# Streaming encoder step: weight products by pairs of column groups, and a dense weight matrix laid out for direct use as stationary operand

## The reference, cut to what matters

```
z = rmsnorm(x) @ w_in; h = x + mixers(z) @ w_out        # retention and mLSTM heads
q = rmsnorm(h) @ w_q;  s1, s2 = q against keys1, keys2   # 8 heads, 128 keys each
pick 16 best (i1, i2) pairs per head -> expert e = i1 * 128 + i2, with a gate
h += sum over picked e of gate * gelu(u[e] . x) * v[e]   # 128 experts per token, of 16384
h += sigmoid(rmsnorm(h) @ w_ple_gate) * (p @ w_ple_proj); y = rmsnorm(h)
```

## Time and profile before

| | |
|---|---|
| time, three runs | 3791.88, 3810.11, 3811.25 us; median 3810.11 |
| the profiled execution: its time, its span | 3817.56 us, 3815.7 us |
| mean granted TensorE clock | 0.899 |
| PE busy | 3148.9 us (83%) |
| DVE busy | 2762.2 us (72%) |
| ACT, POOL busy | 679.6 us (18%), 1329.1 us (35%) |
| moved | 1470.90 MB, mean 385 GB/s |

### The profile page before, as it was taken

How to read it: one execution, slowest core, us unless ns; L and a number is a source line. 1 busy time by engine, 2 the same in 40 slices (tenths; PEclk the granted TensorE clock), 3 DMA queues, 4 the chain that set the end, 5 groups by cost and what they waited for, 6 DMA issues and landing times.

```text
span 3815.7 us, 27395 instructions
## 1 busy us (share of the span) xinstructions
PE 3148.9 (83%) x9486; PEld 1696.0 (44%) x9486; DVE 2762.2 (72%) x3853; ACT 679.6 (18%) x1648; POOL 1329.1 (35%) x905
## 2 busy tenths in 40 slices
PE   8998697998885559999888645699999999888927
PEld 4447343544464234454437635344444444343403
DVE  1005987677677778878757788878788999787772
ACT  2212110222020221123202457000000000011003
POOL 0001533224235444423333522433333333246460
PEclk9999798999997769999998756899999999998968
DMA  7889999999999999999899999999999999999995
GB/s 268 283 274 342 418 417 418 417 418 419 416 398 414 390 362 417 417 417 397 328 402 408 377 365 337 357 420 420 420 420 420 420 419 412 411 417 397 413 370 185
DMA packets 333059, 1470.90 MB, mean 385 GB/s; under 512 B 28152, under 2 KB 66488, under 8 KB 198712
## 3 DMA queue, kind: packets, MB, share of 16 engines
q0 software_dynamic: 129744, 944.82, 60.6%
q1 hardware_dynamic: 192528, 512.40, 35.3%
q10 hardware_dynamic: 10648, 11.92, 1.0%
HBM read 1443.36 MB, written 25.69 MB: 385 GB/s over the span
## 4 chain that ended last, share of the span: by engine, by line
DMA 41%; PE 24%; DVE 9%; issue 5%; POOL 5%; ACT 3%; SPq 0%; DVEq 0%; ACTq 0%; POOLq 0%
DMA ring<-in_peer_v,eidx 21%; PE psum L830 13%; DMA ring<-in_peer_u,eidx 9%; POOL ring L766 5%; DMA W<-in_w_peer_q 5%; PE psum L808 4%; DVE ring L2135 3%; DVE arena L2147 3%; PE psum L1076 2%; PE psum L1139 2%; DMA a_scratch<-arena 1%; DMA W<-in_w_out 1%; DMA W<-in_w_ple_gate 1%; PE psum L1109 1%; PE psum L1194 1%
## 5 line engine op out<-in xcount | busy, mean ns | idle before, releaser
L766 POOL DMA_INDIRECT ring<-in_peer_u,eidx x576 | 879.6, 1527 | 1739.4 <-DVE dots L2135 1310.1
L2135 DVE CUSTOM_DVE_ANT_0 ring<-ring,cx 128x2048 f32<-128x2048 f32 x576 | 1312.1, 2285 | 207.5 <-DMA ring<-in_peer_u,eidx 205.5
L2147 DVE SCALAR_TENSOR_TENSOR arena<-ring,wts,arena 128x2048 f32<-128x2048 f32 x320 | 751.8, 2349 | 210.7 <-DMA ring<-in_peer_v,eidx 194.4
L830 PE MATMUL psum<-W,actT 128*128 128x512 f32 x1792 | 785.9, 597 | 14.0 <-DVE arena L1891 10.6
L766 POOL DMA_INDIRECT ring<-in_peer_v,eidx x320 | 446.3, 1395 | 632.6 <-DVE arena L2147 595.1
L830 PEld LDWEIGHTS psum<-W,actT 128*128 128x128 f32 x1792 | 339.7, 192 | 428.2 <-issue 417.2
L1139 PE MATMUL psum<-arena 128*128 128x512 f32 x1024 | 455.2, 605 | 22.1 <-DVE arena L2058 22.1
L808 PE MATMUL psum<-W,actT 128*128 128x512 f32 x960 | 432.3, 607 | 40.1 <-issue 28.0
L1139 PE MATMUL psum<-W,arena 128*128 128x512 f32 x1024 | 447.2, 596 | 8.7 <-DVE arena L2058 8.7
L1076 PE MATMUL psum<-actT,W 128*128 128x128 f32 (+2 forms) x1536 | 289.9, 354 | 82.8 <-DMA W<-in_w_peer_q 71.4
L1139 PEld LDWEIGHTS psum<-arena 128*128 128x128 f32 x1024 | 197.6, 195 | 269.6 <-issue 239.4
(11 more groups left out here) (283 smaller groups left out, 2149.1 us busy)
## 6 DMA issues: line engine op xcount, KB each, us to landing
W<-in_w_in SPq DMA_DIRECT2D x168, 1024.0 KB, 12.8
W<-in_peer_v SPq DMA_DIRECT2D x64, 1024.0 KB, 14.9
arena<-in_peer_v SPq DMA_DIRECT2D x64, 1024.0 KB, 17.6
W<-in_w_out SPq DMA_DIRECT2D x48, 1024.0 KB, 13.0
W<-in_w_peer_q SPq DMA_DIRECT2D x48, 1024.0 KB, 23.0
W<-in_w_ple_gate SPq DMA_DIRECT2D x48, 1024.0 KB, 16.3
actT<-a_scratch SPq DMA_DIRECT2D x64, 256.0 KB, 26.7
ring<-in_peer_u,eidx POOLq DMA_INDIRECT x576, 16.3
```

What stands on the lines that cost most here:

```text
L766: pool.indirect_dma_start(ring[:, slot, :], None, a["peer_u" if what == "u" else "peer_v"][0], off(ix, 0)).then_inc(ring_in[slot], 16)
L830: ins = pe.matmul(bank(4 * s + j), lhs(at_k, j), w_pair(q)[:, k, s * CG:(s + 1) * CG], start=(at_k == 0), stop=(at_k == KT - 1))
L2135: dve.tensor_tensor_reduce(row, row, cx[:, :], 1.0, 0.0, ALU.mult, ALU.add, dots[:, n % DEEP, c:c + 1]).then_inc(u_used, 1)
L2147: dve.scalar_tensor_tensor(out=hslot(t), in0=ring[:, slot, :], scalar=wts[:, n % DEEP, c:c + 1], in1=hslot(t), op0=ALU.mult, op1=ALU.add). ...
```

## The change

Five edits. `q` of g = 1, 2 and `ple` of e = 0, 1 are done by pairs too, with their places on ACT and DVE moved to where both groups of a pair are done (`done_at`, `group_at`, and the first pick from 1.5 to 2.6 units behind the start of `q`). The turned last quarter of `h` goes to other banks (`h_bank`). The operands of the build product change sides, so that A has the second index on partitions. A is written by transfers of 1 MB (16 tokens, two stages), in a scratch layout of 16 chunks, each with 8 KB in a piece for every second index; a chunk of 8 first indices is read back by one transfer of 1 MB. The dense product takes its stationary operand straight from the chunk, with a step of 8 elements (32 bytes) between tokens; transposes and their copies are gone.

```diff
-CHUNK = 4
+CHUNK = 8
+NCHUNK = NKEY // CHUNK
+WRITE = 4
...
 def paired(what, g):
-    return g > 0 and what in ("in", "out")
+    return g < 2 if what == "ple" else g > 0
...
     if i == j == 0:
-        return q_at(g, 1.5) + FIRST_PICK[g] * x
+        return q_at(g, 2.6) + FIRST_PICK[g] * x
...
 def group_at(e, i, x):
-    return embed_at(e, 4 + 2.2 * len(EMBEDS[e]) * (i + 1)) + x
+    n = len(EMBEDS[e])
+    if paired("ple", e):
+        return embed_at(e, 4 + 2.2 * n * (2 * (i // 2) + 2)) + n * (i % 2) + x
+    return embed_at(e, 4 + 2.2 * n * (i + 1)) + x
...
-        a_keep = nc.dram_tensor("a_scratch", (TOKENS, NKEY * NKEY), F32, kind="Internal").ap()
+        a_keep = nc.dram_tensor("a_scratch", (NCHUNK, NKEY, TOKENS, CHUNK), F32, kind="Internal").ap()
...
-                sp.wait_ge(a_c, b + 1)
-                sp.dma_start(a_keep[b * BATCH:(b + 1) * BATCH, :].rearrange("t (i k) -> i t k", i=NKEY),
-                             a_stage(b).rearrange("p (t k) -> p t k", t=BATCH)).then_inc(a_out[b % 4], 16)
+                sp.wait_ge(a_c, WRITE * (w + 1))
+                t0 = w * WRITE * BATCH
+                sp.dma_start(a_keep[:, :, t0:t0 + WRITE * BATCH, :].rearrange("c i t k -> i c (t k)"),
+                             a_stage(w).rearrange("p c t k -> p c (t k)")).then_inc(a_out[w % 2], 16)
...
                     if c >= 2:
-                        sp.wait_ge(at_tr, (c - 1) * CHUNK // VT)
-                    for b in range(len(DENSE)):
-                        sp.dma_start(a_chunk(c)[:, b, :], a_keep[b * P:(b + 1) * P, c * CHUNK * NKEY:(c + 1) * CHUNK * NKEY]
-                                     ).then_inc(chunk_in[c % 2], 16)
+                        sp.wait_ge(d_done, 4 * (m - 2))
+                    sp.dma_start(a_chunk(c).rearrange("p t k -> p (t k)"), a_keep[c].rearrange("i t k -> i (t k)")
+                                 ).then_inc(chunk_in[c % 2], 16)
...
         def pe_pairs(pe, what, g, n, lhs, room, at, side, beside=None):
...
+                    if beside and step == 2 * WQ - 1:
+                        for s in range(2):
+                            for j in range(0 if s else 1, n):
+                                beside(i + s, j)
...
-                    ins = pe.matmul(bank(b % 4)[:, x * P:(x + 1) * P], hot1(b)[:, x, :], hot2(b)[:, x, :], start=True, stop=True)
+                    ins = pe.matmul(bank(b % 4)[:, x * P:(x + 1) * P], hot2(b)[:, x, :], hot1(b)[:, x, :], start=True, stop=True)
...
-                            ins = pe.matmul(bank(at % 3 * 2 + half), a_turned(m)[:, i // 2, x, :], v_tiles(m)[:, x, c0:c0 + 512],
+                            ins = pe.matmul(bank(at % 3 * 2 + half), a_chunk(c)[:, i // 2 * P:(i // 2 + 1) * P, m * VT % CHUNK + x], v_tiles(m)[:, x, c0:c0 + 512],
                                             start=(x == 0), stop=(x == VT - 1))
```

More of the change, by code:

```diff
@@ L582, in build @@
         ring_in = [sem(f"ring_in{i}") for i in range(8)]
[L583 to L586, removed]
+        split, index_t, index_c, away, hots1, hots, a_mm, a_c, d_done, d_add = (
+            sem("d_" + x) for x in ("split", "index_turned", "index_copied", "away", "hots1", "hots2", "a_mm", "a_copied",
+                                    "product", "added"))
+        a_out = [sem(f"d_a_out{i}") for i in range(2)]
         chunk_in, tiles_in = [sem("d_chunk0"), sem("d_chunk1")], [sem("d_tiles0"), sem("d_tiles1")]
@@ L795, in pe_product @@
             if paired(what, g):
-                pe_pairs(pe, what, g, n, lhs, room, at, side)
+                pe_pairs(pe, what, g, n, lhs, room, at, side, beside)
                 return side
@@ L817, in pe_product, with pe_pairs @@
             return side
-        def pe_pairs(pe, what, g, n, lhs, room, at, side):
+        def pe_pairs(pe, what, g, n, lhs, room, at, side, beside=None):
             for i in range(0, ZG if what == "in" else DG, 2):
@@ L824, in pe_pairs @@
                     for s in range(2):
+                        if beside and step == 2 * WQ - 1 and s == 0:
+                            beside(i, 0)
                         for j in range(n):
@@ L1016, in pe_out_side, with h_bank @@
                 pe_h_turn(pe, g, q)
+        def h_bank(g, q):
+            return (2, 6, 6, 4)[q] if g else (2, 6)[q % 2]
         def pe_h_turn(pe, g, q):
@@ L1062, in score @@
                     ins.then_inc(scored, 1)
+            if paired("q", g):
+                for i in range(0, DG, 2):
+                    for step in range(2 * WQ):
+                        U, q = prod.use0["q", g] + i + step // WQ, step % WQ
+                        pe.wait_ge(landed[q], 16 * (U + 1))
+                        if i == 0 and step % 2 == 0:
+                            pe.wait_ge(n_cp, counts.quarter0["ffn", g] + (step // 2 + 1) * n)
+                        if i == step == 0:
+                            pe.wait_ge(added, DG * b0 + 3 * n)
+                        if i and step == 0:
+                            score(i - 2)
+                        for s in range(2):
+                            for c in range(4):
+                                if i and step == 0 and c % 2 == 0:
+                                    pe.wait_ge(q_taken, HH * g + 4 * (i - 2 + s) + c + 2)
+                                for k in range(2):
+                                    at_k, at = 2 * step + k, c % 2 * MAXB * P
+                                    ins = pe.matmul(bank(2 * s + c // 2)[:, at:at + fresh],
+                                                    w_pair(q)[:, k, s * CG + c * P:s * CG + (c + 1) * P], actT[:, at_k, 0:fresh],
+                                                    start=(at_k == 0 and c % 2 == 0), stop=(at_k == KT - 1 and c % 2 == 1))
+                                if step == 2 * WQ - 1:
+                                    ins.then_inc(mm, 1)
+                        if step < 2 * WQ - 1:
+                            ins.then_inc(used[q], 1)
+                        if i == 0 and step < 2:
+                            pe_h_turn(pe, g, DG - 2 + step)
+                        if i and step == 0:
+                            score(i - 1)
+                score(DG - 2)
+                score(DG - 1)
+                return
             for i in range(DG):
@@ L1497, in scores @@
                         ins.then_inc(s_taken, 1)
+                together = 2 if g else 1
+                for i in range(0, DG, together):
+                    for x in range(together):
+                        yield from take_q(i + x)
+                    for x in range(together):
+                        yield from take_scores(i + x)
             def move():
```

86 lines of the change are left out of this document (34 added, 52 removed).

## The result

The changed kernel takes 3823.82 us (median of 20 runs, 3808.32 to 3838.24), the kernel before 3810.14 us (20 runs). The ratio is 1.0035, 95% interval 1.0022 to 1.0047: slower by 13 us, where I had forecast 24 us less. That is inside the 0.5% that I had called no change and inside the range of 3760 to 3826, but on the wrong side.

What follows compares the result with a forecast made beforehand. The prediction took the DMA transfers, plus the holes between them, to bound the kernel. Its terms -14 - 12 - 5 + 8 gave -23 us, 3787 from the median; it said 3786 us, range 3760 to 3826.

Steps and rivals of the forecast that it cites:

- Second embedding by pairs: Second embedding: DVE reaches the second pair about 12 us early and stalls, the ring hides part; +8, from 0 to +25.
- E of the prediction: Pair boundaries in the two embeddings and two `q` stall more than 8 us; 3817 us, chance 0.08.
- Cheaper packets: Wider rows make four products' weights (10.7 us) and the chunks of A (4.0 us) cheaper to transfer; -14.
- Holes filled: First embedding and `q`: weights arrive faster, DVE waits less, holes in the transfers fill; -12, bounds 0 and 12.
- rival B: Only packets count; holes stay or move, DVE waits as long at its later place; 3804 us, chance 0.22.
- Start of the dense product: Head of the dense product: without transposes, a copy and a second chunk PE starts about 5 us sooner; -5, 0 to -9.
- Transposes gone: Dense product's steps: dropping 256 transposes and 32 copies gains 0, since DVE's next add stands behind 8 gathers.
- Stationary with a step of 32 bytes: Dense product: strided stationary loads stay hidden under the products, costing 0 below 489 ns an instruction.
- Writes of A: Building A: same 512-byte runs, same number, so cost unchanged; 0, from 0 to +56 for the new HBM layout.
- rivals C and D: C: writes of A get slower, 3843 us, chance 0.10. D: strided stationary slow, PE bounds dense product, 4382 us, chance 0.08.
- Loads of `q` at 140 GB/s or more: Expected in the changed kernel's profile: weight loads of `q` run at 140 GB/s or more.
- The other three terms: Cheaper packets -14, Holes filled -12 and Start of the dense product -5.

Runs made afterwards that it cites:

- ple1_retimed: Changed kernel, all pairs kept, second embedding's first pair 2.1 rows earlier and second 1.2 rows later in DVE's order; 3812.28 us, ratio 1.0006 to before.
- ple1_single: Changed kernel with the second embedding by single column groups again, the first still by pairs; 3798.67 us, ratio 0.9972 to the kernel before.
- q_pairs_only: Kernel before with only the two `q` products by pairs, embeddings and dense part as before; 3810.7 us, ratio 0.9992; timed once more (_again), 0.9995.

## Why the prediction was wrong, point by point

**The step that failed: "Second embedding by pairs", +8, bounds 0 to +25.** The mechanism, its place and its sign were right, the size was not: stage 528 to last v is 26.6 us longer, just past the upper bound. The first wait came as worked out. PE began the second pair at 3557.7 and the multiply could run at 3634.2; DVE's 22 gathers took 64 us where I had 71, and it stood 10.45 us where I had said about 12. (My sum says 82 + 4 and 71, which is 15, not 12.)

Two errors lie behind it. I stopped at the first wait; three more followed in the same pair, 8.23, 2.28 and 3.22 us, because multiply, projection and sigmoid of a pair's six results hand over to each other: 24 us in all. And I counted on the ring of 6 rows to hide up to 15 us. It did hide the waits of single groups. DVE's waits for results of the embedding, 3400 to 3720, before:

```profile
DVE arena L2078 <- PE psum L1194: 12.2, 6, 3.9
DVE arena L2078 <- ACT arena L1591: 4.5, 2, 2.3
```

and after:

```profile
DVE arena L2112 <- PE psum L1225: 17.2, 4, 8.2
DVE arena L2112 <- ACT arena L1625: 12.7, 2, 10.5
```

Before, none is above 3.9 us, and from row 528 to 575 the transfers were full. After, the sum is 13 us larger, most of it falls in 43 us of time, and from row 528 to 575 the transfers left 24 us unfilled (one window of it: (1.01 - 0.75) x 50 = 13 us at 3650 to 3700). The other half of the 26.6 us lies in DVE's waits for gathers, 53.9 us in the stage in place of 41.5. The stage grew by more than the stall of 24 us, so these numbers show none of it hidden.

The rival that came true was E of the prediction, "pair boundaries stall more than 8", 3817, which I gave 0.08, though at one of its four boundaries only; a boundary whose own bound was three times its value deserved more.

**Cheaper packets, -14: right, and nearly so in its parts.** Summed over the trace, q1 took 1347.7 us of the engines before and 1333.6 after: -14.1. The four products took 179.0 us before and 168.9 after (the packets of 4 KB beyond those before), 10.0 less (forecast 10.7). The chunks took 44.2 us for 16.8 MB before (2.64 us a MB in 2300 to 3320, as the weights of the earlier trace rows); at the 2.39 of 8 KB rows beside them now they take 40.1, 4.1 less (forecast 4.0). The writes cost 2.2 more, which I had at 0, and some 2 us are scatter of packets that the change doesn't touch, so that the total fits so well is partly luck. The cheaper chunks reached the time: 28 steps save 28/32 x 4.1 = 3.6 us by this sum, and rows 416 to 528 are 4.9 us shorter. But "it needs no engine to do anything in time" was false for the 3 us of the second embedding: there DVE stood for results, and even in ple1_retimed the stage is 5 us longer than with single groups.

**Holes filled, -12: a quarter of it.** Around 2155, in rows 320 to 368, the unfilled time went from 4.0 to 1.1 us, and DVE's wait of 10.8 us is gone; but the stage takes 168.1 us where it took 169.1. DVE's longest waits from 2000 to 2480, in the changed kernel:

```profile
DVE ring L2169 <- DMA ring<-in_peer_u,eidx: 41.3, 26, 5.9
```

The kernel before has 23.4 us there in 16 waits. In rows 320 to 368 alone DVE waits 17 to 18 us for gathers in each of the eleven profiles with `q` by pairs and 10 to 11 in each of the three without: it waits for gathers where it had waited for `q`. That a weight stream with wider packets takes its larger share from the gathers fits this, but no run isolates it. Row 272 to 320 is 6 us shorter, yet not by a hole: it was full before and after, and 5.7 us less of transfer time falls into it. In the first embedding three stalls became two, and their sum grew. Waits of DVE, 1000 to 1450:

```profile
DVE arena L2112 <- ACT arena L1625: 39.3, 2, 26.3
```

against 31.3 us, where I had forecast none above 5 us. That was rival B's mechanism ("DVE waits at the later place as long as it did at the earlier"), with 0.22. The unfilled time up to row 272 grew by 13 us in this pair of profiles, part of it scatter.

**Start of the dense product, -5: right in direction.** The first product ran 17 us earlier in the execution:

```profile
2401.23 29.25 PE L1170 MATMUL psum<-W,actT 128*128 128x512 f32 x64 [20.11 <-DMA actT<-a_scratch]
```

DVE waited 2.7 us for it in all, not 18.0. Rows 368 to 416 are 12.6 us shorter; with the dense part alone 10 and 4 us, so this profile is past the bound of -9 and the -5 is within the three; as the `q` pairs alone shorten the stage by 5 to 6 too, the two can't be told apart here. The unfilled time fell by 8 us.

**Transposes gone, 0 inside the steps: right.** Rows 416 to 528 are 4.9 us shorter over 28 steps, 0.2 us each, though each step lost 8 transposes and a copy; the cheaper chunk alone accounts for 0.13 of it. PE idles 700 - 640 = 60 us in the window at 2500 to 3200, 2.7 a step of 31.6.

**Stationary with a step of 32 bytes, 0: right.** The group of the changed kernel, busy us and mean ns:

```profile
L1170 PEld LDWEIGHTS psum<-W,arena 128*128 128x128 f32 x512 | 159.6, 314 | 75.6 <-DVE arena L2092 10.3 <-issue 9.6
```

314 ns in place of 191 to 196 at the same granted clock (0.98 and 0.99), below the 431 of a product. This is the side of the rule of the Trainium skill that the prediction weighed (SBUF — State Buffer, the note on cachelines): the trace agrees that such an access costs, 1.6 times here, and shows that it costs nothing under a product. A step's products still take their 27.63 us:

```profile
2578.87 27.63 PE L1170 MATMUL psum<-W,arena 128*128 128x512 f32 x64
```

**Writes of A, 0: right.** Queues of the changed kernel from 2310 to 2400, against the earlier trace rows:

```profile
q1 hardware_dynamic: 15556, 8.88, 33.3%
```

0.333 x 90 / 8.88 = 3.38 us a MB (3.34 before). The prediction's rivals C and D both fell.

**Loads of `q` at 140 GB/s or more: not reached.** From 1040 to 1110:

```profile
q1 hardware_dynamic: 2335, 9.00, 32.1%
```

9.00 MB in 70 us is 129 GB/s, at 2.50 us a MB; the price held, the share of the queue was less than in the earlier trace rows.

Put together, from the first two lines of the table: -1.5 + 9.1 - 6.2 - 1.0 - 12.6 - 4.9 + 26.6 - 0.8 = +8.7 us between the two profiled executions, where the forecast had -23. Without the one boundary the forecast's sign holds: the changed kernel with single groups there gives 0.9972, 11 us less than before, and with both embeddings single 0.9958 and 0.9956, 16 us less. That last is the lowest ratio found, though its interval overlaps that of ple1_single. The other three terms had promised 31 us: besides the boundary, "Holes filled" was too large.

## What to carry to other kernels

When work is made coarser under a fixed order, lay out every hand-over of a portion, not only the first wait, and move the places in the order with it: 3.3 rows of distance were worth 21 us in their stage here, nearly as much as all that the change saved in other stages (24 us). A ring that hides waits of up to 4 us spread over a stage need not hide 24 us of them in a row. Price a term in the stage where it falls. And look at the rows behind a hole before you count it as filled: here waits for `q` turned into waits for gathers.

## What the runs showed of the hardware that was not expected

Packets of one size have different prices in different stages. In the kernel before, 2 KB rows took 2.94 us a MB in the first 500 us, 2.63 to 2.72 from 1000 to 3640 beside the gathers (the chunks of A among them, 2.64), and 2.81 after 3640. What sets this wasn't tried. The first 45056 of these packets, which no edit touches, took 270.7 to 280.7 us of the engines in the fourteen profiles. So totals of one packet size can't be subtracted between kernels to price a few us; only packets of one stage can.

Runs of 256 bytes cost 4.43 us a MB and runs of 512 bytes 3.44: half the run is 1.3 times the price, 18 ns an engine against 28.

One wait differs between executions of code that no edit touches. DVE waits for the denominators ahead of row 272, before and in q_pairs_only_again, 1800 to 1850:

```profile
DVE dens L1840 <- PE psum L978: 21.9, 1, 21.9
```

```profile
DVE dens L1892 <- PE psum L988: 10.1, 1, 10.1
```

From 1750 to 1930 the longest such wait is 9.8 and 10.1 us in two profiles, whose stage 128 to 272 took 600 and 595 us, and 19.9 to 27.4 in the other twelve, where it took 606 to 615. Two of the profiles are of one and the same kernel (q_pairs_only and q_pairs_only_again: 26.8 and 10.1 us), and their stages differ by 18 us. That is more than the effect of this change; only stages, many profiles, or medians of many runs could be compared.
